# A two-layer block with diff attention, MLA and retention: the retention projections dealt out in quarters over the MLA steps

## The reference

```python
h = _rms_norm(x, attn_norm[layer])
(d_q, d_k, d_v, m_cq, m_ckv, m_krope, r_q, r_k, r_v, r_g) = _split_cols(h @ w_in[layer])
o_diff = _diff_attention(d_q, d_k, d_v, ...)        # 4 heads, two softmaxes each
o_mla = _mla(m_cq, m_ckv, m_krope, ...)             # 4 heads, causal softmax, 64+32 wide keys
o_ret = _retention(r_q, r_k, r_v, r_g, ...)         # 4 heads, chunks of 128 tokens, a running state
x = x + jnp.concatenate([o_diff, o_mla, o_ret], axis=-1) @ w_out[layer]
h = _rms_norm(x, ffn_norm[layer])
x = x + (jax.nn.silu(h @ w_gate[layer]) * (h @ w_up[layer])) @ w_down[layer]
```

## Time and profile before

| | us |
|---|---|
| median of 3 runs | 2683.39 |
| lowest and highest of them | 2674.73, 2686.8 |
| span of the profiled execution | 2675.5 |
| PE busy in it | 2538.8 |
| from the end of the first layer's MLA scores of step 1 (356.46) to its step 31 output product (537.44) | 180.98 |

### The profile page before, as it was taken

How to read it: one execution, slowest core, us unless ns; L and a number is a source line. 1 busy time by engine, 2 the same in 40 slices (tenths; PEclk the granted TensorE clock), 3 DMA queues, 4 the chain that set the end, 5 groups by cost and what they waited for, 6 DMA issues and landing times. The chain is left out here.

```text
span 2675.5 us, 43064 instructions
## 1 busy us (share of the span) xinstructions
PE 2538.8 (95%) x13054; PEld 2177.0 (81%) x13054; DVE 1533.2 (57%) x3045; ACT 1094.8 (41%) x2503; POOL 1013.6 (38%) x1161
## 2 busy tenths in 40 slices
PE   6999989999899999999989999999998999999997
PEld 5999967878688888888889998777786888888886
DVE  4666555482655454577656665454727445445885
ACT  4444554272522232344444445433624322223444
POOL 2455432173254545201044555221823444441012
PEclk9999999999999999999989999999999999999999
DMA  5111011023233233573331101011222333236633
GB/s 180 29 34 36 19 37 38 12 81 142 71 110 101 91 110 109 183 257 99 99 110 32 35 19 41 5 38 59 89 102 63 114 107 113 82 110 240 210 97 122
DMA packets 238651, 242.68 MB, mean 91 GB/s; under 512 B 27904, under 2 KB 171008, under 8 KB 238464
## 3 DMA queue, kind: packets, MB, share of 16 engines
q1 hardware_dynamic: 238464, 240.43, 27.8%
HBM read 172.75 MB, written 67.63 MB: 90 GB/s over the span
## 5 line engine op out<-in xcount | busy, mean ns | idle before, releaser
L2414 POOL TENSOR_TENSOR fw_a_lo<-fw_a_raw,fw_a_hi 128x512 fp32r<-128x512 f32 x132 | 179.5, 1360 | 467.9 <-DVE fw_s_raw L1997 467.9
L2414 POOL TENSOR_TENSOR fw_s_lo<-fw_s_raw,fw_s_hi 128x512 fp32r<-128x512 f32 x176 | 229.3, 1315 | 52.0 <-ACT fw_s_hi L1487 52.0
L723 PE MATMUL banks<-ht_hi,da_hi 128*128 128x512 f32 x496 | 192.9, 389 | 0.0
L723 PE MATMUL banks<-ht_lo,da_hi 128*128 128x512 f32 x496 | 192.9, 389 | 0.0
L723 PE MATMUL banks<-ht_hi,da_lo 128*128 128x512 f32 x496 | 192.9, 389 | 0.0
L723 PE MATMUL banks<-w_diff_hi,ht_hi 128*128 128x384 f32 x512 | 179.7, 351 | 6.4 <-DVE ht_lo L1674 4.4
L723 PE MATMUL banks<-w_diff_hi,ht_lo 128*128 128x384 f32 x512 | 171.9, 336 | 0.0
L723 PE MATMUL banks<-w_diff_lo,ht_hi 128*128 128x384 f32 x512 | 171.5, 335 | 0.0
L2242 POOL TENSOR_TENSOR qk_rot<-rope_a,rope_b 128x512 f32<-128x512 f32 x64 | 82.6, 1291 | 207.1 <-DVE rope_b L1703 207.1
L1731 DVE TENSOR_REDUCE stats<-banks 128x1 f32<-128x1024 f32 (+3 forms) x192 | 138.3, 748 | 32.3 <-PE banks L924 27.4
L723 PE MATMUL banks<-h_t_hi,fw_s_hi 128*128 128x512 f32 x352 | 139.9, 398 | 13.2 <-DVE h_t_lo L2001 8.2
(11 more groups left out here) (357 smaller groups left out, 7474.9 us busy)
## 6 DMA issues: line engine op xcount, KB each, us to landing
da_raw<-act_scratch SPq DMA_DIRECT2D x154, 256.0 KB, 2.6
fw_a_raw<-in_w_gate_dram SPq DMA_DIRECT2D x88, 256.0 KB, 3.1
act_scratch<-act_s SPq DMA_DIRECT2D x66, 256.0 KB, 2.9
w_diff_raw<-in_w_in_dram SPq DMA_DIRECT2D x24, 512.0 KB, 5.8
fw_a<-in_w_up_dram SPq DMA_DIRECT2D x44, 256.0 KB, 3.2
fw_a_raw<-in_w_up_dram SPq DMA_DIRECT2D x44, 256.0 KB, 2.9
act_scratch<-act_zero SPq DMA_DIRECT2D x44, 256.0 KB, 2.4
act_scratch<-act_one SPq DMA_DIRECT2D x44, 256.0 KB, 2.8
```

The lines of the kernel that those rows point to most:

```text
L723: mm = pe.matmul(bank, lhsT, rhs, start=first and i == 0, stop=last and i == len(pairs) - 1, skip_group_check=resumes)
L2414: pool.tensor_tensor(w[1][:], w[2][:], w[0][:].bitcast(F32), ALU.subtract).then_inc(S["f_lo"], 1)
```

## The change

A unit's projection can be split in four quarters of two row blocks each (6 products), which are dealt over steps by `RET_QUARTERS`: (start, counts...) gives for one unit the first step and how many quarters each step takes. The quarters of a step are halved again over the two places, ahead of and behind `mla_probs`; a single one goes behind. Steps 1 to 6, 10 to 12, 20 to 22 and 26 to 28 take two quarters, steps 8, 9, 18, 19, 24 and 25 one, and steps 7, 13, 14, 23, 29, 30 and 31 four. GpSimd releases each low part of the retention weights by itself (`w_low` counts them), and the first tile of a pair waits for the part that its quarter needs. `ROUND_RET` becomes (-2, 16): two parts of the first pair are rounded ahead of step 0. The clock-keeping products begin at step 32 instead of 30. `load_out(0)` and the three small loads move from behind unit 25's store to behind unit 28's, the small ones first. All four parts of the output weights are rounded in retention steps 1 to 4, and GpSimd's low parts of them come in steps 2 to 9.

```diff
+def w_low(chunk, part=PARTS - 1):
+    earlier = chunk + (PARTS - 1) * max(0, min(chunk - CH_RET, RET_PAIRS))
+    return earlier + (part + 1 if CH_RET <= chunk < CH_OUT else 1)
...
-        ret_unit_at = {(7 if n < T else 13) + n: n for n in range(RET_UNITS)}
-        ROUND_RET = (0, 16)
+        RET_QUARTERS = [(1, 2, 2), (3, 2, 2), (5, 2, 2), (7, 4), (8, 1, 1, 2), (11, 2, 2), (13, 4), (14, 4),
+                        (18, 1, 1, 2), (21, 2, 2), (23, 4), (24, 1, 1, 2), (27, 2, 2), (29, 4), (30, 4), (31, 4)]
+        ret_quarters_at, ret_unit_at = {}, {}
+        for n, (start, *counts) in enumerate(RET_QUARTERS):
+            for i, count in enumerate(counts):
+                ret_quarters_at[start + i] = [(n, sum(counts[:i]) + q) for q in range(count)]
+            ret_unit_at[start + len(counts) - 1] = n
+        ROUND_RET = (-2, 16)
...
-        ROUND_OUT = {0: 2, 2: 3}
+        ROUND_OUT = {1: 0, 2: 1, 3: 2, 4: 3}
...
-                        if h * T + T - 1 - t == 25:
+                        if h * T + T - 1 - t == 28:
                             sp.wait_ge(S["z_done"], L * PER["z_done"] + Z_UNITS)
-                            load_out(0)
                             arrives(causal[:], causal_dram, "ret_in")
                             arrives(gn_w[:], ret_gn_w[L].partition_broadcast(P), "ret_in")
                             arrives(gn_b[:], ret_gn_b[L].partition_broadcast(P), "ret_in")
+                            load_out(0)
...
-                def ret_project(a, part):
-                    if a in ret_unit_at:
-                        n = ret_unit_at[a]
-                        project(Z_RET + n, n % T, CH_RET + n // T, w_ret, 4 * P, (part,))
+                def ret_quarter(n, q):
+                    t, chunk = n % T, CH_RET + n // T
+                    if t == 0:
+                        pe.wait_ge(S["w_hi"], L * PER["w_hi"] + PARTS * chunk + q + 1)
+                        pe.wait_ge(S["w_lo"], L * PER["w_lo"] + w_low(chunk, q))
+                    if q == 0:
+                        pe.wait_ge(S["z_free"], L * PER["z_free"] + Z_RET + n)
+                    pairs = [pair for k in (2 * q, 2 * q + 1) for pair in
+                             split((ht_hi[:, k, tokens(t)], ht_lo[:, k, tokens(t)]), (w_ret[0][:, k, :], w_ret[1][:, k, :]))]
+                    mm = products(banks[:, Z_BANK, :], pairs, first=q == 0, last=q == 3)
+                    if q == 3:
+                        mm.then_inc(S["z_done"], 1)
+
+                def ret_project(a, slot):
+                    quarters = ret_quarters_at.get(a, [])
+                    for n, q in quarters[len(quarters) // 2:] if slot else quarters[:len(quarters) // 2]:
+                        ret_quarter(n, q)
...
-                    if a == MLA_UNITS - 2:
+                    if a == MLA_UNITS:
                         pe.wait_ge(S["z_free"], L * PER["z_free"] + Z_UNITS)
...
-                    if a >= MLA_UNITS - 2:
+                    if a >= MLA_UNITS:
                         keep_clock(1)
...
+                weights(CH_RET, range(-ROUND_RET[0]))
...
                     if a > MLA_UNITS:
-                        n = a - MLA_UNITS - 1
-                        ret_gate_and_v(n)
-                        weights(CH_OUT, [n])
+                        ret_gate_and_v(a - MLA_UNITS - 1)
...
-                        if i == PARTS - 1:
+                        if i == PARTS - 1 or CH_RET <= chunk < CH_OUT:
                             st.then_inc(S["w_lo"], 1)
...
-                    if u < KD:
-                        out_low(u)
+                    if 0 <= u - 2 < KD:
+                        out_low(u - 2)
```

More of the change, by code:

```diff
@@ L114, in mla_back_rings @@
     return back
+def w_low(chunk, part=PARTS - 1):
+    earlier = chunk + (PARTS - 1) * max(0, min(chunk - CH_RET, RET_PAIRS))
+    return earlier + (part + 1 if CH_RET <= chunk < CH_OUT else 1)
 PER = dict(
     params_in=16 * 8, ret_in=16 * 3, x_saved=16, x_back0=16, x_back1=16, mix_in=16,
-    w_in0=16 * (3 + 3 + 1 + 4 + 4 + 1), w_in1=16 * (3 + 3 + 4 + 1), w_gain=1, w_hi=PARTS * CHUNKS, w_lo=CHUNKS,
+    w_in0=16 * (3 + 3 + 1 + 4 + 4 + 1), w_in1=16 * (3 + 3 + 4 + 1), w_gain=1, w_hi=PARTS * CHUNKS, w_lo=w_low(CHUNKS - 1),
     lam=5, n_sq=2 * T, n_ms=5, n_rstd=5, n_xn=2 * T, tr_done=RING, tr_hi=RING - NORM2_RINGS - MLA_HEADS * T, tr_free=RING - 1,
@@ L760, in project @@
                         pe.wait_ge(S["w_hi"], L * PER["w_hi"] + PARTS * (chunk + 1))
-                        pe.wait_ge(S["w_lo"], L * PER["w_lo"] + chunk + 1)
+                        pe.wait_ge(S["w_lo"], L * PER["w_lo"] + w_low(chunk))
                         if u > T:
@@ L860, in mla_up @@
                     pe.wait_ge(S["w_hi"], L * PER["w_hi"] + CH_UKV + 1)
-                    pe.wait_ge(S["w_lo"], L * PER["w_lo"] + CH_UKV + 1)
+                    pe.wait_ge(S["w_lo"], L * PER["w_lo"] + w_low(CH_UKV))
                     if u >= 2:
@@ L1079, in first_blocks @@
                         pe.wait_ge(S["w_hi"], L * PER["w_hi"] + PARTS * (CH_OUT + 1))
-                        pe.wait_ge(S["w_lo"], L * PER["w_lo"] + CH_OUT + 1)
+                        pe.wait_ge(S["w_lo"], L * PER["w_lo"] + w_low(CH_OUT))
                     products(banks[:, t, :], out_pairs(0, t, range(KD - 2)))
@@ L1121, in _ @@
                             pe.wait_ge(S["w_hi"], L * PER["w_hi"] + PARTS * (CH_OUT + 2))
-                            pe.wait_ge(S["w_lo"], L * PER["w_lo"] + CH_OUT + 2)
+                            pe.wait_ge(S["w_lo"], L * PER["w_lo"] + w_low(CH_OUT + 1))
                         pe.wait_ge(S["out_add"], L * PER["out_add"] + q - 3)
```

## The result

The changed kernel takes 2715.09 us (median of 4 runs, 2708.96 to 2722.42) against 2680.61 for the kernel before on the same chip: ratio 1.0127, 95% interval [1.0109, 1.0145]. It is slower by 34 us where I forecast 7.6 faster, and outside my range of 2664 to 2688. The profiled execution has a span of 2707.2 us, 31.7 above the 2675.5 of before.

A forecast was written before the change was run, and what follows sets the result against it. The prediction took TensorE, busy 95% of the first part, as the bound. It summed -17.9 (steps), +6.9 (drain), +1.0 (clock) and +2.4 (retention) to -7.6 us: 2675.8 us from a median of 2683.4, range 2664 to 2688.

The forecast's parts named there:

- The clock: At the start of retention, a 4.8 us stall lowers PE's clock: 0.5 us a layer, between 0 and 2; +1.0 in all.
- The steps up to 31: Attention steps 1 to 31: projection quarters fill PE's idle time, -9.0 us a layer, -17.9 us in all.
- The waits for weights at steps 2 and 20: PE waits there for late low parts of the retention weights: 1.0 and 1.2 us, ends 0 and 2.4.
- The drain: Before the first state product, a store held behind the 2 MB load delays GpSimd and PE: +3.9 and +2.9 us.
- The retention stage: GpSimd's later low blocks delay PE at step 10: 1.2 us a layer, between 0 and 2.9; +2.4 in all.
- (a): Rival: stores slip past the load or GpSimd's wait ends in time, so the drain is cheap; 2667.9 us, chance 0.22.
- (b): Rival: PE loses its clock waiting for weights in steps 2 and 20, costing 11.2 us; 2687.0 us, chance 0.10.
- (c): Rival: only recorded idle in the attention steps can be filled, 4.0 us a layer; 2685.7 us, chance 0.13.

The follow-up runs named there:

- e11: e8 with 8 more clock-keeping products in each of retention units 10 and 11, unit 10's ahead of its wait: 2688.61 us, ratio to before 1.0025.
- e13: e8 with 8 more clock-keeping products in each of retention units 11 and 12, behind the wait at unit 10: 2696.36 us, ratio to before 1.0052.
- e8: Kernel before with only GpSimd's eight low blocks of the output weights moved to retention steps 2 to 9 from 0 to 7: 2714.69 us, 1.0122.
- e4: Changed kernel with the 2 MB load behind the last store, roundings in retention steps 2 to 5, low blocks in 3 to 8: 2725.01 us, 1.0146.
- e6: Kernel before with all the change's edits to drain and retention stage, no projection moved: 2721.88 us, 1.0152.
- e5: Kernel before with only the first head pair's projections in quarters, steps 1 to 14; drain and retention code untouched: 2669.72 us, 0.9959.
- e2: Changed kernel with the low blocks of the output weights in retention steps 2 to 7 instead of 2 to 9: 2709.59 us, 1.0107.
- e3: Changed kernel with 20 clock-keeping products ahead of each stage's first state product and low blocks in retention steps 2 to 7: 2690.23 us, 1.0027.
- e7: e4 with roundings in retention steps 3 to 6 and low blocks in steps 4 to 8, 16, 18 and 20: 2722.82 us, 1.0157.
- e9: e7 with the mixed rows transposed in retention steps 7 to 18 instead of 5 to 16: 2688.35 us, 1.0011.
- e12: e9 with the low block of retention step 8 moved to step 15: 2666.66 us, 0.9948.

## Why the prediction was wrong

**The clock was the failed step.** I put it at 0.5 us a layer, between 0 and 2, "where products are small". Measured in the changed kernel: 19.1 us in the first layer's stage, which has no other wait, and some 14 in the second's (15.7 less the 1.7 by which its second wait, 2.40, is longer than the old one of 0.67). The place was right, and so was the reason for expecting trouble there, but I took small products for a small price. It is the reverse. e11 and e13 against e8 show it: 16 dense products a layer, ahead of the wait or behind it, are worth 26 and 18 us. The Trainium skill, "TensorE: Matmul & The Clock Gate", section "What's actually happening", says that the throttled state is the default and activity releases it. I weighed that against steps 2 and 20, where full quarters stand on both sides of the wait, and not against the stage with the thinnest products. By e13 the trace agrees with it. In the same traces PE's bars are full for 30 to 67 us at 0.50: a full bar was not enough.

**The steps up to 31: right in kind, 9.0 forecast and 6.9 measured.** By windows of the first layer, forecast and measured: steps 1 to 6 +11.9 and +11.3; 7 and 8 -4.1 and -3.3; 9 -4.2 and -2.9; 10 to 12 -8.2 and -8.3; 18 to 20 +4.4 and +4.5; 21 to 24 -9.9 and -9.1; 25 to 28 -12.5 and -12.9; 29 to 31 +13.8 and +13.7. What is missing is where a step keeps one quarter or gives them all up: step 9 waited 1.02 us for its exponential and 0.96 for VectorE, of which I had the first alone. The waits for weights at steps 2 and 20 were 0.61 and 1.16 (forecast 1.0 and 1.2). A slip of the sum itself: 54 products are 12.3 us and not 12.5, and the terms as written add up to -8.8 a layer, not -9.0.

**The drain: right mechanism, mis-sized.** Forecast +3.9 and +2.9, measured +5.5 and +4.0. The store was released late as described (7.52 us of GpSimd). The load left 3.34 and 4.60 us behind the output product (forecast 3.7). Its landing, in us from issue, in the two layers:
```profile
w_o_raw<-in_w_out_dram SPq DMA_DIRECT2D x1, 2048.0 KB, 9.5
...
w_o_raw<-in_w_out_dram SPq DMA_DIRECT2D x1, 2048.0 KB, 9.3
```
I had taken 7.7 for the first layer, so the missing 1.6 us there are the landing, and the missing 1.1 in the second mostly the later issue (0.9). e4 shows the cause: the load behind the stores, and the drain is 9.81.

**The retention stage: right place, wrong price.** GpSimd was late where the earlier trace rows said it would be, PE's wait growing from 0.76 to 2.40. I sized it at 1.2 a layer, at most 2.9. e8, the same edit alone, costs 13.1 and 14.1 of stage, 1.6 of it the wait. In these runs such costs don't add: in the changed kernel's first layer the clock is already down and GpSimd's lateness shows no wait at all, and e6, with two more waits of over 6 us than e8, is only 7 us slower.

**The rivals.** (a), a cheap drain, was false. (b) named the right mechanism at the wrong place: the waits of 0.61 and 1.16 us did not lower the clock among full quarters (0.98 over the steps, as before). Its price was too high as well: behind the gap of the earlier trace rows nine products of 512 columns ran slow in the kernel before, not 14, and e5 shows 1.6 us for such a fall where I had 2.8. (c) was false by the windows above. No rival put the clock into the retention stage, and none reached 2715.

**Left open.** Why the second layer of the changed kernel had its clock back some 5 us behind a wait of 5.50 us while the first needed 50 behind 4.47, on the same code: e2 repeats the late return in both layers, e6 the early one in both. Three late returns (the changed kernel's at 595, e2's second at 1931, e3's at 1905) stand right behind the same place, the first tile of the second head pair, which has no state to multiply and so fewer small products; but e4 and e7 passed it at 0.50. Neither do the runs say why e9 ranges over 27 us; that the wait of 1.47 us drops the clock in some executions and not in others would do it, but only one was profiled.

## What to carry to other kernels

Before moving work in a stage of small matmuls, list every wait of TensorE there and what stands in order ahead of its releaser on GpSimd, ScalarE and the DMA queues; a wait of one to two microseconds that costs little beside dense products (nothing or some 1.6 us more here, e5) can cost ten to thirty among small ones (11.5 in e9's first stage, 28.5 in e4's). Where it can't be removed, put a few clock-keeping products ahead of it (e11), or a dense burst right behind it (e13). Read PE's busy bars only beside the granted clock: in e8 full bars at 0.50 took 30 us for what takes 18.5 at 1.00.

## What the hardware showed that I had not expected

- A granted clock of 0.50 held for 67.25 us with PE busy in every microsecond of it (e4), and came back within one burst of nine 512-column products in both layers of e13.
- In the retention stage it fell at every profiled wait that was not filled and took 1.47 to 6.40 us, in e4 at the second of a pair (1.34, then 1.04), and at 0.85 us in one case, where 0.96, 0.85 and 0.84 in others left it at 1.00. In steps 2 and 20, 0.61 and 1.16 us among quarters left it alone; the wait of 1.65 us among whole projections dropped it in 6 of 14 places.
- Two loads that overlap, 2 MB and 3 MB, moved some 400 GB/s together (397 in e4's window), as one alone does (404 to 410 in the kernel before). In e4, e7, e9 and e12 the 2 MB, issued first, landed 7.7 to 8.0 us after issue, as when alone (7.7 in the earlier trace rows), and the 3 MB after 15.7 to 15.9 instead of 10.4: here the second paid for both.
